# A two-layer hybrid trunk on one core: natural row order, the first projection row tile by row tile, and the last weight split behind each softmax

## The reference, cut to what matters

```
h = h + short_conv_mixer(rms_norm(h, norm_mix[0]), ...)        # layer 0
h = h + hierarchical_moe(rms_norm(h, norm_ffn[0]), ...)
h = h + dilated_attention_mixer(rms_norm(h, norm_mix[1]), ...)  # layer 1
h = h + hierarchical_moe(rms_norm(h, norm_ffn[1]), ...)
out = rms_norm(h, norm_final)
# rms_norm:  y = x * rsqrt(mean(x*x) + eps) * g
# attention: qkv = x @ w_qkv (1024 x 9216); three head groups with dilation 1, 4, 16;
#            16 heads of 64, rotary q and k, softmax within each group, merged by log-sum-exp
# moe:       16 experts (4 groups of 4), top 2 of the chosen group;
#            out += combine[:, e] * ((silu(t @ w_gate[e]) * (t @ w_up[e])) @ w_down[e])
```

## Time and profile before

| | |
|---|---|
| median of 3 runs | 1548.24 us (1543.72 to 1548.25) |
| profiled execution, its own time | 1546.9 us |
| span of its trace | 1545.2 us |
| mean granted TensorE clock | 0.941 of full speed |
| busy, share of the span | PE 88%, PEld 72%, DVE 63%, ACT 49%, POOL 13% |
| experts of layer 0 and of layer 1 | about 250 to 541 us, and 1218 to 1512 us |
| attention proper (`attend`) | about 782 to 841 us, and 1054 to 1112 us |

### The profile page before, as it was taken

How to read it: one execution, slowest core, us unless ns; L and a number is a source line. 1 busy time by engine, 2 the same in 40 slices (tenths; PEclk the granted TensorE clock), 3 DMA queues, 4 the chain that set the end, 5 groups by cost and what they waited for, 6 DMA issues and landing times.

```text
span 1545.2 us, 20454 instructions
## 1 busy us (share of the span) xinstructions
PE 1363.3 (88%) x7161; PEld 1119.1 (72%) x7161; DVE 977.9 (63%) x1196; ACT 751.1 (49%) x835; POOL 203.7 (13%) x301
## 2 busy tenths in 40 slices
PE   5999955999999929999988999998886599999991
PEld 4888734888888718888867888887774488888870
DVE  6445364999999773252456535246736489899983
ACT  4222142788888631422264142226513278878871
POOL 4000011111111121120200202020001111111112
PEclk9999976999999959999999999999998699999995
DMA  6232354999999552223210222320044289999964
GB/s 207 82 122 95 123 198 145 348 385 390 390 390 392 227 208 88 90 87 109 82 56 1 82 82 82 101 91 28 1 177 171 80 327 392 392 386 389 391 254 174
DMA packets 83596, 301.94 MB, mean 195 GB/s; under 512 B 12091, under 2 KB 12115, under 8 KB 67156
## 3 DMA queue, kind: packets, MB, share of 16 engines
q1 hardware_dynamic: 74036, 283.86, 49.7%
q0 software_dynamic: 9504, 17.33, 2.9%
HBM read 293.28 MB, written 25.17 MB: 206 GB/s over the span
## 4 chain that ended last, share of the span: by engine, by line
PE 84%; DVE 7%; ACT 3%; DMA 2%; issue 2%; POOL 1%; POOLq 0%; SPq 0%; DVEq 0%; ACTq 0%
PE ps L298 25%; PE ps L300 24%; PE ps L299 24%; PE ps L1500 2%; PE ps L1348 1%; DVE hn L849 1%; PE ps L1486 1%; PE ps L1550 1%; PE ps L1454 1%; DMA x_rows<-hn_rows,tok_list 1%; ACT prob L729 1%; DVE probT L1173 1%; PE ps L1305 1%; ACT square_out L598 1%; PE ps L1471 1%
## 5 line engine op out<-in xcount | busy, mean ns | idle before, releaser
L298 PE MATMUL ps<-W_hi,xT_hi_all 128*128 128x512 f32 x1408 | 561.8, 399 | 18.7 <-DVE xT_lo_all L990 9.6
L300 PE MATMUL ps<-W_hi,xT_lo_all 128*128 128x512 f32 x1408 | 553.3, 393 | 0.0
L299 PE MATMUL ps<-W_lo,xT_hi_all 128*128 128x512 f32 x1408 | 552.4, 392 | 0.0
L982 DVE TENSOR_TENSOR W_lo<-m_raw,W_hi 128x2048 fp32r<-128x2048 f32 x192 | 435.6, 2291 | 65.2 <-ACT W_hi L623 65.2
L623 ACT ACTIVATE W_hi<-m_raw 128x2048 fp32r<-128x2048 f32 x192 | 367.0, 1914 | 45.7 <-PE ps L300 44.7
L816 DVE TENSOR_TENSOR W_lo<-raw,W_hi 128x2048 fp32r<-128x2048 f32 x56 | 135.1, 2414 | 312.3 <-ACT W_hi L592 312.2
L298 PEld LDWEIGHTS ps<-W_hi,xT_hi_all 128*128 128x128 f32 x1408 | 266.7, 189 | 77.1 <-issue 7.3
L300 PEld LDWEIGHTS ps<-W_hi,xT_lo_all 128*128 128x128 f32 x1408 | 266.8, 189 | 57.9
L299 PEld LDWEIGHTS ps<-W_lo,xT_hi_all 128*128 128x128 f32 x1408 | 267.4, 190 | 52.7
L592 ACT ACTIVATE W_hi<-raw 128x2048 fp32r<-128x2048 f32 x56 | 107.1, 1914 | 369.0 <-PE ps L300 367.9
L572 POOL TENSOR_TENSOR qk_rot<-rope_a,rope_b 128x512 f32<-128x512 f32 x48 | 61.8, 1290 | 399.4 <-DVE rope_b L1234 399.2
(11 more groups left out here) (207 smaller groups left out, 1333.4 us busy)
## 6 DMA issues: line engine op xcount, KB each, us to landing
m_raw<-in_w_gate_dram SPq DMA_DIRECT2D x64, 1024.0 KB, 7.8
m_raw<-in_w_up_dram SPq DMA_DIRECT2D x64, 1024.0 KB, 8.6
m_raw<-in_w_down_dram SPq DMA_DIRECT2D x64, 1024.0 KB, 8.4
raw<-in_attn_w_qkv_dram SPq DMA_DIRECT2D x36, 1024.0 KB, 5.0
raw<-in_conv_w_in_dram SPq DMA_DIRECT2D x12, 1024.0 KB, 5.1
y_pick<-y_rows SPq DMA_DIRECT2D x16, 512.0 KB, 7.4
raw<-in_conv_w_out_dram SPq DMA_DIRECT2D x4, 1024.0 KB, 5.0
hn_rows<-hn SPq DMA_DIRECT2D x8, 512.0 KB, 2.6
```

The costliest lines, as they stand in the source:

```text
L298: pe.matmul(o, a_hi, b_hi, start=first, stop=False)
L299: pe.matmul(o, a_hi, b_lo, start=False, stop=False)
L300: return pe.matmul(o, a_lo, b_hi, start=False, stop=last)
L982: dve.tensor_tensor(MW_lo[c % MSPLIT][:, :, :], m_raw[c % MRAW][:, :, :], MW_hi[c % MSPLIT][:, :, :].bitcast(F), ALU.subtract).then_inc(s[ ...
```

## The change

1. `norm_row` reads and writes `h`, `gain` and `hn` in natural order for all stages. PE picks the permuted blocks instead: the stationary operand of the transposes in `turn_rows` and `turn_x` is read with a step of eight elements (32 bytes).
2. The split of unit U_QKV+7 of group 2 (`hi` and `lo`) moves behind the exponentials: ACT does it before its wait for `gap_in`, DVE behind `scales`. One exponential of a 128 x 1 tile is added on ACT in group 2, behind the copies of part p = 1.
3. The first projection part of s = 0 (units 0 and 1) is computed by `first_rows`: per row tile both halves of the contraction, in the order (0,0) (0,1) (1,0) (1,1) (2,0) (3,0) (2,1) (3,1) of (row tile, half).
4. SP issues `later_weights(0)` before the first three w_qkv units.

```diff
@@ SP
             norm_gain(2)
+            later_weights(0)
             for j in range(3):
                 qkv_unit(j, 0, 0)
-            later_weights(0)
@@ ACT, attend
+                hi(U_QKV + 7, s * 3 + 2)
                 act.wait_ge(gap_in, s + 1)
@@ ACT, projection loop
-                        hi(U_QKV + 2 * p + 3, rev)
+                        if g == 2 and p == 1:
+                            act.activation(exp_of_half[:, :], neghalf[:, :], ACT.Exp)
+                        if g < 2 or p < 2:
+                            hi(U_QKV + 2 * p + 3, rev)
@@ DVE, norm_row
-                if first < 16:
-                    o = hn[r % 2][:, :].rearrange("p (k q) -> p k q", k=KD)
-                    i0 = h[:, r, :].rearrange("p (q k) -> p k q", k=KD)
-                    i1 = gain[:, :].rearrange("p (q k) -> p k q", k=KD)
-                else:
-                    o, i0, i1 = hn[r % 2][:, :], h[:, r, :], gain[:, :]
-                dve.scalar_tensor_tensor(out=o, in0=i0, scalar=rstd[:, r:r + 1], in1=i1, op0=ALU.mult,
-                                         op1=ALU.mult).then_inc(hn_ready, 1)
+                dve.scalar_tensor_tensor(out=hn[r % 2][:, :], in0=h[:, r, :], scalar=rstd[:, r:r + 1],
+                                         in1=gain[:, :], op0=ALU.mult, op1=ALU.mult).then_inc(hn_ready, 1)
@@ DVE, attend
                 scales(s)
+                lo(U_QKV + 7, s * 3 + 2)
@@ DVE, projection loop
-                        lo(U_QKV + 2 * p + 3, rev)
+                        if g < 2 or p < 2:
+                            lo(U_QKV + 2 * p + 3, rev)
@@ PE, turn_rows
-                        rows = hn_r[r % 2][:, k * P:(k + 1) * P]
+                        rows = hn_r[r % 2][:, k::KD]
@@ PE, turn_x
-                                           x_rows_r[:, k * P:(k + 1) * P], ident_r[:, :])
+                                           x_rows_r[:, k::KD], ident_r[:, :])
@@ PE, before the projection loop
+            def first_rows():
+
+                for r, kh in ((0, 0), (0, 1), (1, 0), (1, 1), (2, 0), (3, 0), (2, 1), (3, 1)):
+                    if r == 0:
+                        pe.wait_ge(split_lo, RAW + U_QKV + kh + 1)
+                    if kh == 0:
+                        pe.wait_ge(v_ready, r + 1)
+                        pe.wait_ge(x_lo, 8 + r + 1)
+                    for k in range(4):
+                        ...
+                        ins = product(pe, ps[:, r, :], ...)
+                    if r == NT - 1:
+                        ins.then_inc(unit_done, 1)
+                    elif kh == 1:
+                        ins.then_inc(qkv_done, 1)
```

More of the change, by code:

```diff
@@ L164, in build @@
         head_scale = keep("head_scale", [P, 2, NT, 8])
+        exp_of_half = keep("exp_of_half", [P, 1])
         cos_t = keep("cos_t", [P, NT, HD])
@@ L1520, in attend @@
                 weighted(15, s)
+            def first_rows():
[6 more added lines that the diff above has]
+                    for k in range(4):
+                        xh, xl = xT_hi_all[:, 4 * kh + k, :], xT_lo_all[:, 4 * kh + k, :]
+                        ins = product(pe, ps[:, r, :], xh[:, r * P:(r + 1) * P], xl[:, r * P:(r + 1) * P],
+                                      W_hi[kh][:, k, :], W_lo[kh][:, k, :], kh == 0 and k == 0, kh == 1 and k == 3)
+                    if r == NT - 1:
+                        ins.then_inc(unit_done, 1)
+                    elif kh == 1:
+                        ins.then_inc(qkv_done, 1)
             for s in range(2):
@@ L1524, in _ @@
                     for p in range(3):
+                        if s + g + p == 0:
+                            first_rows()
+                            continue
                         for kh in range(2):
@@ L1530, in _ @@
                                     pe.wait_ge(v_ready, (s * 3 + g) * 4 + r + 1)
-                                    pe.wait_ge(x_lo, 8 + r + 1)
                                 elif kh == 0:
```

## The result

The changed kernel takes 1537.14 us (median of 5 runs, 1536.06 to 1538.29), the one before 1547.49 (5 runs): ratio 0.994, 95% interval 0.9926 to 0.9954. I had forecast 1563 us, slower. The profiled execution took 1538.29 us, its span is 1536.5 us against 1545.2.

A forecast was written before the change was run, and what follows sets the result against it. PE was taken as the bound, without idle time in the experts. 26.4 - 1.9 - 7.3 - 2.0 + 0.5 = +15.7 us gave 1562.6 us, slower; forecast range 1551 to 1573, wide range 1530 to 1578.

The forecast's parts named there:

- The price of a transpose with a step: In `turn_x` and `turn_rows`: each transpose that PE reads with a step costs 0.097 us more.
- The term of 26.4 us: Experts: 272 `turn_x` transposes on PE's path at 0.097 us each, paid in full.
- the other side: Rival for PE's transposes: the step is free, -15.2 us, 1531.7 us, faster; chance 0.36.
- my own sum: Whole kernel: 318 (272 + 46) times the price per transpose, less 15.2 us of other terms; forecast +15.7 us.
- the norm's ratio put on PE's own spacing: PE's transposes: 2.06 / 1.28 = 1.6 on 0.077 us, 0.047 us more each; as rival 1546.6 us, chance 0.06.
- The two DVE rows that agreed: DVE's excess with a step: norm 0.76 ns per element, reduce 0.58; for 128 elements 0.097 and 0.074 us.
- The turns ahead of the projections: `turn_rows`: 8 x 0.097 = 0.78 us more per row tile, leaving 1.9 of the norms' 6.4 us.
- the walk through the stretches: Shorter norms at the start, before both routers and after the first experts: 6.4 us saved with transposes at the old price.
- Part 2: Split moved behind the softmax: exponentials 4.3 and 3.0 us earlier, 7.3 us saved, plus 2.0 us from the clock.
- First rows: First projection: no wait removed, PE waits for the first rope, 0.5 us lost (bounds 0 and 1.5).
- Queue order: w_qkv units behind the last expert weights: zero at both ends, up to 3 us if a scatter met them.
- the estimate from it: PE's stepped loads, by 16-byte lines: 0.227 us per load instead of 0.077, making the sum +32.5 us.

The follow-up runs named there:

- part 1 alone: Only natural row order in `norm_row`, with stepped transposes in `turn_rows` and `turn_x`, against the kernel before: 1548.07 us against 1546.7, ratio 1.0006.
- part 3 alone: Only the first projection part computed row tile by row tile by `first_rows`, against the kernel before: 1546.87 us against 1546.7, ratio 1.0001.

## Why the prediction was wrong

- *The price of a transpose with a step* is the step that failed. "I take 0.097 us" was DVE's excess per element moved to PE; measured are 0.049 us per load and 0.039 us per transpose in the item's period. The term of 26.4 us measured 10.1 us (6.4 + 3.7; 10.2 in part 1 alone, 10.5 by the period). The point from which I let the other side win was 0.048 us; with 0.039 my own sum is 318 x 0.039 - 15.2 = -2.8 us, so the size of this one term turned the sign. That 1537 us lie within my wide range (1530 to 1578) is no merit of the sum, as that range holds both signs. The bounds, 0 and 0.18 us, were right, and so was the place: PE pays in full, having no idle time in the experts. The nearest value among those I listed was the one that I set aside, the norm's ratio put on PE's own spacing (0.047 us); that it came near is no proof of its reason, which no run tests. The two DVE rows that agreed said nothing of PE, and their agreement was weaker than I took it for: the reduce with the step also writes 16 sums and the one without it 4, so the 37 ns between them are not the step's alone.
- *The turns ahead of the projections.* I charged the full-clock price (0.78 us a turn) where the engine runs at the lower clock; measured are 0.07 us there, and 0.38 us in the two turns at the upper clock. Of the 6.4 us that the norms could save I kept 1.9; the trace shows 1.1 + 3.7 + 1.8 = 6.6 us, more than my 6.4 even behind the price of the turns, so the walk through the stretches was too low as well. With both corrected my own sum is 10.1 - 6.6 - 9.3 + 0.5 = -5.3 us: faster. Most of what is still missing to the -8.7 us of the spans are 2.2 us of clock in part 2.
- *Part 2* was right in mechanism: 4.2 and 2.9 us at the starts against 4.3 and 3.0, and 4.2 us in the two softmax stretches, where the clock now stays up, against 2.0 (bounds 0 to 6.8). I took the added exponential for 1.3 us; left out, it costs 1.2 us in the chain and 2.6 us behind it with the lower clock.
- *First rows*: 0.5 us lost was forecast, 0.56 us are in the trace of part 3 alone; nothing in the time. The rest of the +1.2 us in the table is the clock at the start of that projection, which kernels without `first_rows` show too (35.1 to 36.2 us for this stretch).
- *Queue order*: zero, as forecast.
- *DMA in the experts.* I expected its busy share at about 92%. It stays at 1.00 (400 to 520 us, before and after); what falls is the rate, from 389 to 383 GB/s.
- *Lines of 16 bytes.* The Trainium skill's page "SBUF — State Buffer" (the note on cachelines, in Door 1) ties the price to steps beyond a 16-byte line: by that, 2 elements should have been cheap. Here a step of 8 bytes costs a load as much as one of 32 (195 and 188 ns). And the estimate from it, 0.227 us per load, is not what the trace shows. The Trainium skill's page "TensorE: Matmul & The Clock Gate" (LDWEIGHTS) counts a load by its columns alone. The trace doesn't bear that out either: 139 and 188 ns for 128 columns at one clock.

What stays open: why a load with a step takes longer in a turn, and why one with two or four elements' step takes 7 to 10 ns more than one with eight; and the 1 to 3 us by which experts and attention stretches of kernels with the same code in them differ, with dips of the clock at changing places (experts without a step 298.7 to 302.1 us, with the step of eight 305.3 to 305.7, all with the old layout of the weights).

## What to carry to other kernels

A price taken from another engine is a bound and not a value: when the sign hangs on it, give both signs the weight that the bounds give them. Here the step of a transposed operand was paid at full clock and in the stream without idle time (0.35 us a turn); in the short turns at the lower clock it was nearly free (0.07 us), so such a step is to be tried there first and not in the inner loop. In front of a softmax, move everything off ACT and DVE that the first step doesn't need, the table load included: with PE's gap at 0.68 us instead of 4.8 the clock stayed at its upper level besides. And measure the parts of a change alone: here one of four carried all of the gain that can be told from no change.

## What the runs showed of the hardware

- In a turn of transposes, a stationary load of 128 f32 columns takes 139 ns in order and 188 to 198 ns with a step of 2, 4 or 8 elements at full clock, and the turn of eight takes 0.79 us in order and 1.14 to 1.20 us with a step. At the lower clock loads take 182 ns in order and 187 to 195 with the step of 8. Between 512-column matmuls a load in order takes 188 ns at full clock and is covered; what a step does there no run shows.
- DVE's three-operand norm over 1024 elements takes 1.28 us in order, 2.06 us reading two inputs with a step, 1.96 us writing with one, in runs of eight elements.
- 1 MB weight units in pieces of 2 KB instead of 8 KB lower the DMA rate from 389 to 378 GB/s, with 141708 instead of 83596 packets in the whole run.
- With a gap of 0.67 or 0.68 us in PE's work at the start of an `attend` the granted clock stayed at 2.4 GHz, in every kept trace; with 1.96, 3.55 and 4.8 us it fell to 1.2 GHz for part of what followed.
